# First projection by slices of two feature tiles for all columns, its weight pieces in turn with the ada pieces

## What is computed

```python
mod = silu(c) @ ada_w[0] + ada_b[0]          # shift, scale, ... : 6 x 1024 columns
h = rms_norm(x, pre_mix_g[0]) * (1 + scale) + shift
z = gelu(h @ w_in + b_in)                    # w_in is 1024 x 4096
u, v = z[:, :2048], z[:, 2048:]
v = layer_norm(v, ln_g, ln_b)                # over its 2048 columns
v = einsum('gts,bnsgc->bntgc', tril(w_s), v) + b_s
y = (u * v) @ w_out
```

## Time and profile before

| | us |
|---|---|
| Median of 3 runs | 1915.36 |
| Lowest and highest run | 1908.89, 1915.43 |
| Profiled execution, its own time | 1910.74 |
| Span of the profiled execution | 1909.0 |
| TensorE busy in the span | 1808.1 (95%) |
| Transfers, mean over the span | 190 GB/s |

### The profile page before, as it was taken

How to read it: one execution, slowest core, us unless ns; L and a number is a source line. 1 busy time by engine, 2 the same in 40 slices (tenths; PEclk the granted TensorE clock), 3 DMA queues, 4 the chain that set the end, 5 groups by cost and what they waited for, 6 DMA issues and landing times.

```text
span 1909.0 us, 21848 instructions
## 1 busy us (share of the span) xinstructions
PE 1808.1 (95%) x8926; PEld 1487.9 (78%) x8926; DVE 1169.3 (61%) x1613; ACT 899.7 (47%) x1236; POOL 7.4 (0%) x20
## 2 busy tenths in 40 slices
PE   3999899988999899999999988999999999999998
PEld 2798688868866688888888766888888889768887
DVE  6888787776643755565546683655465555566543
ACT  3444534446544544454445445644354445455442
POOL 0000000000000000000000000000000000000000
PEclk7999899989988999999999988999999999999999
DMA  9767687856422455555455321554555456225551
GB/s 391 274 264 281 245 308 289 306 203 237 180 72 83 154 217 191 187 197 189 166 209 187 114 85 45 188 192 170 191 208 185 171 201 226 95 98 194 180 176 64
DMA packets 54116, 363.42 MB, mean 190 GB/s; under 512 B 5744, under 2 KB 8944, under 8 KB 13056
## 3 DMA queue, kind: packets, MB, share of 16 engines
q1 hardware_dynamic: 52256, 351.47, 50.2%
q0 software_dynamic: 1760, 10.56, 1.4%
HBM read 360.95 MB, written 1.05 MB: 190 GB/s over the span
## 4 chain that ended last, share of the span: by engine, by line
PE 86%; DVE 6%; ACT 4%; DMA 2%; issue 1%; SPq 0%; DVEq 0%; ACTq 0%
PE pp L575 82%; DMA raw<-in_w 2%; DVE low L1608 2%; PE pp L792 1%; DVE raw L1621 1%; ACT wh L1154 1%; PE pp L730 1%; PE pp L861 1%; ACT hf L1238 0%; ACT junk L1187 0%; DVE tb L1611 0%; DVE x L1611 0%; DVE tb L1608 0%; ACT tb L1338 0%; ACT hh L1224 0%
## 5 line engine op out<-in xcount | busy, mean ns | idle before, releaser
L1608 DVE TENSOR_TENSOR low<-raw,wh 128x2048 fp32r<-128x2048 f32 (+3 forms) x334 | 638.6, 1922 | 380.2 <-ACT wh L1154 379.4
L1154 ACT ACTIVATE wh<-raw 128x2048 fp32r<-128x2048 f32 (+3 forms) x334 | 534.8, 1616 | 438.0 <-PE pp L575 310.8
L575 PE MATMUL pp<-wh,hh 128*128 128x512 f32 x1312 | 529.7, 404 | 38.8 <-ACT wh L1154 20.5
L575 PE MATMUL pp<-low,hh 128*128 128x512 f32 x1312 | 520.4, 397 | 3.1 <-DVE low L1608 3.1
L575 PE MATMUL pp<-wh,hl 128*128 128x512 f32 x1312 | 520.4, 397 | 0.5 <-DVE hl L1608 0.5
L575 PEld LDWEIGHTS pp<-wh,hh 128*128 128x128 f32 x1312 | 252.3, 192 | 97.7 <-ACT wh L1154 21.5
L575 PEld LDWEIGHTS pp<-wh,hl 128*128 128x128 f32 x1312 | 251.8, 192 | 56.7 <-DVE hl L1608 3.0
L575 PEld LDWEIGHTS pp<-low,hh 128*128 128x128 f32 x1312 | 252.5, 192 | 55.2 <-DVE low L1608 4.1
L575 PE MATMUL pp<-wh,hidh 128*128 128x512 f32 x592 | 231.9, 392 | 0.0
L575 PE MATMUL pp<-wh,hidl 128*128 128x512 f32 x592 | 230.5, 389 | 0.0
L575 PE MATMUL pp<-low,hidh 128*128 128x512 f32 x592 | 230.4, 389 | 0.0
(11 more groups left out here) (201 smaller groups left out, 1310.8 us busy)
## 6 DMA issues: line engine op xcount, KB each, us to landing
raw<-in_w SPq DMA_DIRECT2D x314, 1024.0 KB, 4.8
raw<-in_w SPq DMA_DIRECT2D x24, 768.0 KB, 4.3
gain<-in_w POOLq DMA_DIRECT2D x6, 512.0 KB, 5.6
bT<-in_rel POOLq DMA_DIRECT2D x1, 2048.0 KB, 10.8
cst<-in_csts POOLq DMA_DIRECT2D x1, 1029.0 KB, 9.4
xT<-in_xT SPq DMA_DIRECT2D x1, 1024.0 KB, 6.8
wsT<-in_ws POOLq DMA_DIRECT2D x1, 1024.0 KB, 13.9
binr<-in_bin POOLq DMA_DIRECT2D x1, 1024.0 KB, 16.6
```

The source lines that it names most:

```text
L575: return e.matmul(out, lhsT, rhs, start=start, stop=stop, skip_group_check=True)
L1154: q.then_inc(e.activation(wh[j % NW][:, c], raw[i % NRAW][:, c], ACT.Copy), s_wh, (j, part))
L1608: return e.tensor_tensor(out, a, b, op)
```

## The change

- The stream begins with four rounds of four transfers: ada 4+k, ada k, and two mm pieces. A mm piece of `a_v` is now 2 feature tiles for 1024 columns (the same 1 MB), so p0 and p1 hold features 2k, 2k+1 of all 2048 columns for k = 0, and so on. The opening holds 8 ada and 8 mm pieces; `marks` is shifted, so that among p8 to p23 only p12 to p23 have ada pieces, twelve for twelve.
- PE runs `a_v` with all eight accumulator banks of 512 columns open, feature pair by feature pair. The last pair finishes group by group.
- DVE makes h pair by pair between the pieces. Then it adds the bias in eight halves of 512 columns, with `bn_stats` one group behind. The mask product on wsT ("tri") moves behind the aggregate.
- `v` is normalised on ACT (Identity with scale and bias, from a new small value `less_mean`), ahead of `wh` of p10.
- `spatial_bias` moves into and behind a_u 1 on PE. On DVE both its parts stand between the pieces of a_u 0 and those of a_u 1.
- xT is loaded in two halves ahead of `col`.

```diff
 stream():
+    begin = [("mm", [("a_w_in", (0,), cols(2048 + 1024 * half, 1024))], 2 * k, 2, 1024, ("a_v", half))
+             for k in range(4) for half in range(2)]
-    items = [ada[4], ada[0], ada[5], ada[1], main[0], ada[6], ada[2], ada[7], ada[3], main[1]]
-    ada, main = ada[8:], main[2:]
-    marks = [(0, 0), (4, 0), (22, 12), (56, 36), (74, 44), (100, 48)]
+    for k in range(4):
+        items += [ada[4 + k], ada[k], begin[2 * k], begin[2 * k + 1]]
+    ada = ada[8:]
+    marks = [(0, 0), (4, 0), (16, 12), (50, 36), (68, 44), (94, 48)]
 tensor_program:
-            rows("a_v", 0, h(0), (s_side, ("a_v", 0)))
-            rows("a_v", 1, h(0), (s_side, ("a_v", 1)))
+            for k2 in range(4):
+                for half in range(2):
+                    j = of_group[("a_v", half)][k2]
+                    if k2 < 3:
+                        for k in range(2):
+                            for g in (2 * half, 2 * half + 1):
+                                for m in range(2):
+                                    ins = first_products(j, k, g, m)
+                        q.then_inc(ins, s_mm, ("piece", j))
...
-            rows("a_v", 2, h(0), (s_side, ("a_v", 2)), between=lambda: spatial_bias(0))
-            rows("a_v", 3, h(0), (s_side, ("a_v", 3)), between=lambda: spatial_bias(1))
-            for g in range(2):
-                whole("a_u", g, h(0), (s_gate, ("a_u", g)))
+            whole("a_u", 0, h(0), (s_gate, ("a_u", 0)))
+            whole("a_u", 1, h(0), (s_gate, ("a_u", 1)), between=lambda: spatial_bias(0))
+            spatial_bias(1)
 scalar_program:
+            q.wait_ge(s_side, "less_mean")
+            for a in range(2):
+                q.then_inc(e.activation(v[:, a, :], v[:, a, :], ACT.Identity, bias=less_mean[:, a:a + 1], scale=rstd[:, a:a + 1]),
+                           s_sideact, ("v", a))
 vector_program:
+            for k in range(4):
+                ahead.rest()
+                ahead.rest()
+                if k == 0:
+                    q.wait_ge(s_root, "x0")
+                    q.then_inc(e.reciprocal(rsx[:, :], root[:, :]), s_rs, "x0")
+                first_h(k)
+                ahead.rest()
+                ahead.rest()
+            ahead.upto(9)
...
-            for a in range(2):
-                q.then_inc(e.tensor_scalar(v[:, a, :], v[:, a, :], mv[:, a, 0:1], rstd[:, a:a + 1], ALU.subtract, ALU.mult),
-                           s_side, ("v", a))
+            q.then_inc(stt(less_mean, mv[:, :, 0], -1.0, rstd, ALU.mult, ALU.mult), s_side, "less_mean")
             ahead.group("a_u", 0)
+            spatial_bias(0)
+            spatial_bias(1)
             ahead.group("a_u", 1)
```

More of the change, by code:

```diff
@@ L48, in ffn @@
         add("dn" + tag, down, lead, 22, split(0, 2))
-    add("a_v", "a_w_in", (0,), 8, split(2048, 4))
     add("a_u", "a_w_in", (0,), 8, split(0, 4))
@@ L415, in build @@
         rstd = small[:, 52:54]
+        less_mean = small[:, 54:56]
         prod = small[0:64, 56:58]
@@ L445, in build @@
         s_raw = [signal(f"raw{i}_landed") for i in range(NRAW)]
-        s_ld = {n: signal(n + "_landed") for n in ("c", "col", "xT", "x", "cst", "ws", "bin", "bs", "rel")}
+        s_ld = {n: signal(n + "_landed") for n in ("c", "col", "xT0", "xT1", "x", "cst", "ws", "bin", "bs", "rel")}
         s_gain = signal("gain_landed")
@@ L956, in tensor_program, with first_products @@
             stats("x0")
-            rows("a_v", 0, h(0), (s_side, ("a_v", 0)))
-            rows("a_v", 1, h(0), (s_side, ("a_v", 1)))
+            outs = {}
+            for g in range(3):
+                row_begin("a_v", g, (s_side, ("a_v", g)))
+                for m in range(2):
+                    outs[g, m] = pairs.of(("a_v", g)).rows[:, m, :]
+            for m in range(2):
+                outs[3, m], before = misc.begin(("a_v3", m), (s_side, ("a_v", 3)))
+            q.wait_ge(*before)
+            def first_products(j, k, g, m):
+                w_h, w_l, k0, kt, n = weights(j)
+                at, out = k0 + k, outs[g, m][:, :]
+                c, t = slice(512 * (g % 2), 512 * (g % 2) + 512), slice(128 * m, 128 * m + 128)
+                q.wait_ge(s_wh, j)
+                q.wait_ge(s_hi, ("h", 0, at, m))
+                mm(out, hh[:, at, t], w_h[:, k, c], at == 0, False)
+                q.wait_ge(s_lo, ("h", 0, at, m))
+                mm(out, hl[:, at, t], w_h[:, k, c], False, False)
+                q.wait_ge(s_wl, j)
+                return mm(out, hh[:, at, t], w_l[:, k, c], False, at == 7)
+            for k2 in range(4):
[4 more added lines that the diff above has]
+                            for g in (2 * half, 2 * half + 1):
+                                for m in range(2):
+                                    ins = first_products(j, k, g, m)
+                        q.then_inc(ins, s_mm, ("piece", j))
+                    else:
+                        for g in (2 * half, 2 * half + 1):
+                            for m in range(2):
+                                for k in range(2):
+                                    ins = first_products(j, k, g, m)
+                                q.then_inc(ins, s_mm, ("a_v", g, m))
+                        s_mm.at["piece", j] = s_mm.n
             def spatial_bias(g):
@@ L975, in tensor_program @@
                 q.wait_ge(*before)
-                q.wait_ge(s_side, ("v", 1))
+                q.wait_ge(s_sideact, ("v", 1))
                 for g in range(4):
@@ L1478, in scalar_program @@
             first_root()
-            first_h(range(0, 4))
+            for k in range(4):
+                ahead.upto(2 * k)
+                first_h((2 * k, 2 * k + 1))
+                ahead.upto(2 * k + 1)
+            ahead.upto(9)
             def gelu_v(g):
@@ L1487, in scalar_program @@
             for g in range(4):
-                ahead.group("a_v", g, between=(lambda: first_h(range(4, 8))) if g == 0 else None, ahead=1 if g == 0 else NW)
                 gelu_v(g)
@@ L2026, in odd_fill @@
                 yield from out_steps("odd_out")
[L2029 to L2036, removed]
             def first_h(j):
@@ L2062, in spatial_bias @@
                     q.then_inc(ins, s_side, ("bias", n))
[L2064 to L2077, removed]
-                for a in range(2):
-                    ins = e.bn_stats(bst[:, a, g, :], v[:, a, 512 * g:512 * g + 512])
-                q.then_inc(ins, s_side, ("bn", g))
+            q.wait_ge(s_ld["bin"], 0)
+            for g in range(5):
+                if g < 4:
+                    s, before = tb.begin(("a_v", g), (s_sideact, ("gelu_v", g)))
+                    q.wait_ge(*before)
+                    for m in range(2):
+                        q.wait_ge(s_mm, ("a_v", g, m))
+                        b = pairs.of(("a_v", g)).rows[:, m, :] if g < 3 else misc.of(("a_v3", m))[:, :]
+                        ins = tt(tokens2(s)[:, m, :], b, binr[:, 512 * g:512 * g + 512], ALU.add)
+                    q.then_inc(ins, s_side, ("a_v", g))
+                if g:
+                    q.wait_ge(s_sideact, ("gelu_v", g - 1))
+                    for a in range(2):
+                        ins = e.bn_stats(bst[:, a, g - 1, :], v[:, a, 512 * (g - 1):512 * g])
+                    q.then_inc(ins, s_side, ("bn", g - 1))
             q.wait_ge(s_side, ("bn", 3))
@@ L2083, in vector_program @@
                 q.then_inc(e.bn_aggr(mv[:, a, :], bst[:, a, :, :].rearrange("p g s -> p (g s)")), s_side, ("aggr", a))
+            q.wait_ge(s_ld["ws"], 0)
+            q.wait_ge(s_ld["cst"], 0)
+            q.then_inc(tt(wsT[:, :, :], wsT[:, :, :], bc4(tri[:, :], 16), ALU.mult), s_side, "tri")
             q.wait_ge(s_sideact, "rstd")
@@ L2246, in sync_program @@
             e.dma_start(cact[:, :], c_d.partition_broadcast(128)).then_inc(s_ld["c"].sem, 16)
+            for i in range(2):
+                e.dma_start(xT[:, 4 * i:4 * i + 4, :], x_d.rearrange("(k p) t -> p k t", p=128)[:, 4 * i:4 * i + 4, :]).then_inc(
+                    s_ld["xT%d" % i].sem, 16)
             e.dma_start(col[:, :], col_d).then_inc(s_ld["col"].sem, 16)
-            e.dma_start(xT[:, :, :], x_d.rearrange("(k p) t -> p k t", p=128)).then_inc(s_ld["xT"].sem, 16)
             for i, (kind, off, parts, k0, kt, n, tag) in enumerate(items):
```

4 lines of the change are left out of this document (2 added, 2 removed).

## The result

The changed kernel takes 1916.84 us (median of 20 runs, 1913.60 to 1920.64), the kernel before, run beside it on the same chip, 1910.45 us (median of 20, 1906.12 to 1919.70). The ratio is 1.003, with a 95% interval of 1.002 to 1.0039: slower by 0.3%, inside what was called no change. The profiled execution of the changed kernel took 1915.38 us, its span is 1913.6 us. Against the profiled execution before that is 4.6 us more, by the medians 6.4 us.

What follows compares the result with a forecast made beforehand. PE was taken to bound the kernel, busy 1808.1 of 1909.0 us. The opening's gain is lost again, der comes 2.4 us later: 1910.74 + 2.4 = 1913.1, plus 4.6 to the median, 1917.8 us; range 1905.5 to 1924.5.

Steps and rivals of the forecast that it cites:

- The opening: First a_v pieces on PE: third product at 21.9 instead of 30.4 us, p0 to p3 done at 46.5.
- The gap before p6: PE in a_v: waits 4.7 us for low 6 at 63.1, then restarts p6 at the low clock.
- The end of a_v: DVE's last bias add at 76.7 to 77.9, then statistics, aggregates and tri product; small operations done at 83.3.
- v on ACT: Normalising v on ACT takes 3.7 us for two, v ready at 87.0, delaying p10's copy; low 10 at 91.1.
- The restart at p10: PE waits to 91.1 after four products of p10; the gap was counted too short to lower the clock.
- the second rival: Slower by the clock: low clock also at p10, twice as long at a_u 2; 1923.4 us, chance 0.14.
- bsb ahead of a_u 1: DVE idles about 5 us before the second bsb group, done at 107.1; spt at 116.5 against 119.27 before.
- From spt to the boundary: DVE needs 74.8 us, 10.0 of it from four displaced ada pieces; der at 191.3 by this way.
- The last landing: Boundary's piece after p21 ends at 180.5: landing 7.3 us instead of 4.8, then copy and low, giving 191.9.
- a sign of being right: At the first boundary on DVE: der falls within 3 us of 191.9.
- The rival in which the gain survives: Only PE's own pace counts: spt at 105.7, der at 180.5, 9.0 us early; 1906.3 us, chance 0.20.
- The rival by the clock: PE restarts slowly at p10 too, low level twice as long at a_u 2; p21 5.6 us later, chance 0.14.

Runs made afterwards that it cites:

- c1: Changed kernel with ada pieces from p9 on, v on DVE and second bsb group behind the pieces of a_u 1; 1903.02 us, ratio 0.9949.
- c2: c1 plus POOL loading the bias row at the seventh transfer and its other five tables after the last a_v piece; 1897.58 us, ratio 0.9925.
- c4: Kernel before the change with only v's normalisation moved to ACT; 1910.22 us, ratio 0.999.
- e3: Changed kernel with the second bsb group on DVE behind the pieces of a_u 1 instead of ahead; 1910.26 us, ratio 0.9998.
- e4: Changed kernel with POOL's 5.3 MB of tables, bias row included, issued only when the last a_v piece has landed; 1919.78 us, ratio 1.0045.

## Why the prediction was nearly right, step by step

The median came at 1916.84 against 1917.8 predicted, and no change was the likeliest case. The steps:

- **The opening** (third product 21.9, p0 to p3 done 46.5): measured 22.39 and 46.2. Right. The gap before p6, forecast as 4.7 us with a slow restart, was 0.93 us, because PE stopped at p4 already (1.86 and 2.11 us, then 1.2 GHz until 54): p4 was charged as landed near 42 and its copy started at 45.6. So the waits lay elsewhere than forecast, and in sum they were shorter: PE's last product of `a_v` ends at 75.5, forecast 76.7. What the forecast had wrong here is the sharing of DMA between POOL and the stream, which was counted as a total by 60 us and not piece by piece.
- **The end of a_v** (`less_mean` done 83.3): measured 83.76. It was forecast as PE's pace, the last bias add at 76.7 to 77.9; the add came at 77.25 to 78.4 because DVE had its `low` of p9 only at 71.3, forecast 69.7, and PE was done before it. So DVE set this time, and PE, done with a_u 0 at 87.0 instead of 88.3, had the longer wait at p10.
- **v on ACT**, priced 3.7 for two with bounds 2.6 and 5.5: measured 4.08. Its effect was right in kind: PE has `low` 10 at 92.06, forecast 91.1, and half of this difference was there before `v` began.
- **The restart at p10** was counted as too short a gap to lower the clock, 2.2 us behind four products. It did lower it: 0.51 and 0.64 in the stretches 92 to 96. The second `bsb` group starts at 107.43, forecast 105.0: 0.95 us of that are `low` 10, the other 1.5 the clock. This is the mis-sized term: it was in the second rival, with a chance of 0.14.
- **bsb ahead of a_u 1**: forecast a wait of about 5 us on DVE, measured 5.23. `spt` forecast 116.5, measured 118.87.
- **From spt to the boundary**: forecast 74.8 without waits; 76.88 measured, with waits of 0.74 and 1.54, so 74.6 without. Right. DVE is busy for 69.6 us of it, 91%, where over 95% was named as a sign.
- **The last landing**: forecast 7.3 us, measured 8.44, after p21 ended at 182.74 instead of 180.5. The trace of the kernel before had this number already: the second of the two transfers there landed after 8.4 us.

The sum of it: `der` 191.9 forecast, 195.75 measured, outside the 3 us that were named as a sign of being right. Of the 3.85 us, about 0.5 come from the end of `a_v`, 0.3 from `v`, 0.15 from the hand-over to p10, 1.5 from the clock at p10, and 1.6 from the landing, its issue and the copy behind; 0.2 are given back before the end of p21. So the shift against the kernel before was forecast as 2.4 and was 6.2. The number on record lies nearer to the result than this by luck: it was put on the median of the three runs then shown, 1915.36, and twenty runs of the same kernel have theirs at 1910.45. The base was 4.9 us too high and the shift 4.0 us too small. The rival in which the gain survives (`der` at 180.5) fell on the order and on the opening's transfers: c1, with the order mended, has `der` at 183.29, and c2, with the tables late too, at 175.34. The rival by the clock was right at p10, with a smaller price than it gave: p21 ended 2.2 us later than forecast, not 5.6. At a_u 2 the low level did not last twice as long, but from 120.6 to about 126 us, as forecast.

The Trainium skill (TensorE: Matmul & The Clock Gate, HAM oscillation) says that waits for data between groups of matmuls bring the clock down again each time. The trace agrees at p4, p10 and part 3. Behind the single wait of 0.93 us before p6 the clock is 1.00, so not every wait did it here.

## What to carry to other kernels

A gain on the engine that bounds is paid out only if the work behind it is not held back by order: look at every engine's program order behind the stretch, and ask of each moved operation what stands behind it and who waits for that. Moving work to an emptier engine helps only where it lands behind, not ahead of, what the bound engine waits for. When a change makes the opening compete for DMA, list what else is issued there and which of it is needed by then (here one table of six). And where two transfers are issued together, see which of them is waited for: here the second landed 4.0 us after the first.

## What the runs showed of the chip that was not expected

- An Identity activation of 128x2048 with a scale and a bias read from SBUF took 4.08 us for two (4.09 in c4), a copy of the same shape 3.69. The Trainium skill (ScalarE: Activation LUTs, What ACT_TABLE_LOAD costs) gives each such operand a price of about 93 ns; two of them in two instructions make 0.37 us, an estimate from that page, and the trace's 0.39 agrees. The prediction had taken the price from a range instead.
- Two waits of 2.81 and 1.52 us with four products between them were followed by 1.2 GHz, as was the single one of 3.44 us at the same place in c1 (0.50 from 92 to 94 us). In the changed kernel the clock was still 1.00 in the stretch 90 to 92 that holds the four products; in e3, with nearly the same waits there (2.81 and 1.04 us), it was 0.50 in that stretch already. Behind single waits of 1.86 us (the first before p4) and 1.78 us (part 3 in e3) it was 1.00.
- Two queues with work shared DMA about evenly: from 35 to 45 us POOL's queue moved 2.21 MB of 4.20 in all, and the last of its 5.3 MB landed 24.2 us after its issue. A table of 1 MB alone ahead of the others (`binr` in c2) landed in 7.2 us, fourth in the row (in e4) in 16.8.
